# A hybrid attention block on one core: norm weights turned by PE, and two loads of x issued by ScalarE

## The reference

```python
def _rmsnorm(x, g, eps=1e-6):
    y = x * lax.rsqrt(jnp.mean(x * x, axis=-1, keepdims=True) + eps)
    return y * g

h = _rmsnorm(x, norm_g[layer])               # x (512, 2048), norm_g (2048)
proj = h @ w_in[layer]                       # w_in (2048, 10304)
aq, ak, av, ag, cq, ckv, kr, bg, mg = jnp.split(proj, SPLIT_POINTS, axis=-1)
oa = _diff_attention(...)                    # 8 heads, values of 128
oa = _rmsnorm(oa, a_subln_g[layer], 1e-5) * (1.0 - lam_init)       # a_subln_g (128)
ya = (oa * silu(ag)) @ w_oa[layer]
q  = _rmsnorm(cq,  q_norm_g[layer])  @ w_uq[layer]                 # q_norm_g (512)
kv = _rmsnorm(ckv, kv_norm_g[layer]) @ w_ukv[layer]                # kv_norm_g (512)
ob = _mla_attention(...)
yb = (ob * silu(bg)) @ w_ob[layer]
merged = sigmoid(ga) * ya + sigmoid(gb) * yb
x = x + merged @ w_out[layer]
return _rmsnorm(x, final_g)
```

## Time and profile before

| | us |
|---|---|
| median of 3 runs | 1429.9 (1429.22 to 1430.29) |
| profiled execution, whole | 1429.3 |
| its span, first to last instruction | 1427.5 |
| PE busy | 1413.2 (99% of the span) |
| DVE busy | 1020.0 (71%) |
| ACT busy | 707.1 (50%) |
| POOL busy | 31.5 (2%) |

### The profile page before, as it was taken

How to read it: one execution, slowest core, us unless ns; L and a number is a source line. 1 busy time by engine, 2 the same in 40 slices (tenths; PEclk the granted TensorE clock), 3 DMA queues, 4 the chain that set the end, 5 groups by cost and what they waited for, 6 DMA issues and landing times.

```text
span 1427.5 us, 17881 instructions
## 1 busy us (share of the span) xinstructions
PE 1413.2 (99%) x6604; PEld 1175.1 (82%) x6604; DVE 1020.0 (71%) x1381; ACT 707.1 (50%) x894; POOL 31.5 (2%) x52
## 2 busy tenths in 40 slices
PE   8999999999999999999999999999999999999997
PEld 7888888888888888888888878888888888888886
DVE  6967898798878868677667656666676353478966
ACT  6546334544344456665666667555564222324434
POOL 0000000000000000000000000000000000000000
PEclk9999999999999999999999999999999999999999
DMA  8439576766756543222222434322242444617674
GB/s 300 145 125 316 177 263 186 236 213 212 238 184 207 184 146 83 79 82 81 81 81 82 114 106 133 84 72 66 81 140 74 151 125 152 207 45 247 197 254 172
DMA packets 182976, 218.43 MB, mean 153 GB/s; under 512 B 19456, under 2 KB 133248, under 8 KB 182272
## 3 DMA queue, kind: packets, MB, share of 16 engines
q1 hardware_dynamic: 174304, 197.64, 44.5%
q10 hardware_dynamic: 8608, 19.93, 3.6%
HBM read 195.51 MB, written 22.02 MB: 152 GB/s over the span
## 4 chain that ended last, share of the span: by engine, by line
PE 91%; DVE 3%; DMA 1%; ACT 1%; issue 1%; SPq 1%; POOL 0%; DVEq 0%; POOLq 0%; ACTq 0%
PE duo L2115 28%; PE duo L2117 28%; PE duo L2116 28%; PE duo L2168 2%; DMA start_y<-start_columns 1%; PE duo L2142 1%; PE duo L2145 1%; SPq L610 1%; ACT m_hi L886 1%; PE duo L2159 1%; PE duo L2164 1%; PE duo L2163 1%; PE duo L2160 1%; PE duo L2161 1%; PE duo L2598 0%
## 5 line engine op out<-in xcount | busy, mean ns | idle before, releaser
L1385 DVE TENSOR_TENSOR w_lo<-w_raw,w_hi 128x1024 fp32r<-128x1024 f32 (+1 forms) x116 | 135.3, 1167 | 99.3 <-ACT w_hi L781 98.7
L2115 PE MATMUL duo<-h_hi,w_hi 128*128 128x512 f32 x512 | 201.8, 394 | 0.0
L2117 PE MATMUL duo<-h_hi,w_lo 128*128 128x512 f32 x512 | 199.6, 390 | 0.0
L2116 PE MATMUL duo<-h_lo,w_hi 128*128 128x512 f32 x512 | 199.6, 390 | 0.0
L886 ACT ACTIVATE m_hi<-m_raw 128x2048 fp32r<-128x2048 f32 (+1 forms) x66 | 115.5, 1752 | 144.6 <-PE duo L2117 71.5
L781 ACT ACTIVATE w_hi<-w_raw 128x1024 fp32r<-128x1024 f32 (+1 forms) x118 | 119.2, 1011 | 124.3 <-DMA w_raw<-in_w_ob_dram 65.8
L1502 DVE TENSOR_TENSOR m_lo<-m_raw,m_hi 128x2048 fp32r<-128x2048 f32 (+3 forms) x71 | 141.9, 2001 | 26.9 <-ACT m_hi L886 26.5
L2115 PE MATMUL duo<-m_hi,h_hi 128*128 128x512 f32 x368 | 144.6, 393 | 1.6 <-DVE h_lo L1538 0.9
L2117 PE MATMUL duo<-m_hi,h_lo 128*128 128x512 f32 x368 | 143.3, 389 | 0.0
L2115 PE MATMUL duo<-m_hi,s_hi 128*128 128x512 f32 x320 | 124.5, 389 | 0.0
L2117 PE MATMUL duo<-m_hi,s_lo 128*128 128x512 f32 x320 | 124.5, 389 | 0.0
(11 more groups left out here) (322 smaller groups left out, 2991.0 us busy)
## 6 DMA issues: line engine op xcount, KB each, us to landing
m_raw<-in_w_in_dram SPq DMA_DIRECT2D x110, 512.0 KB, 4.7
w_raw<-in_w_in_dram SPq DMA_DIRECT2D x132, 256.0 KB, 3.0
o_raw<-in_w_out_dram SPq DMA_DIRECT2D x32, 512.0 KB, 5.1
spare<-in_w_in_dram SPq DMA_DIRECT2D x17, 512.0 KB, 4.6
h_raw<-in_w_in_dram SPq DMA_DIRECT2D x17, 512.0 KB, 4.9
w_raw<-in_w_oa_dram SPq DMA_DIRECT2D x32, 256.0 KB, 3.3
sig<-gates SPq DMA_DIRECT2D x8, 1024.0 KB, 6.3
w_raw<-in_w_ob_dram SPq DMA_DIRECT2D x32, 256.0 KB, 3.4
```

The source lines that it names most:

```text
L1385: dve.tensor_tensor(w_lo[:, piece.slot, 0:cols], w_raw[:, piece.slot, 0:cols], w_hi[:, piece.slot, 0:cols].bitcast(F32), ALU.subtract).the ...
L2115: pe.matmul(dst, lhs_hi, rhs_hi, start=start, stop=False)
L2116: pe.matmul(dst, lhs_hi, rhs_lo, start=False, stop=False)
L2117: return pe.matmul(dst, lhs_lo, rhs_hi, start=False, stop=stop)
```

## The change

The four norm weights are loaded as rows into a new tile `g_rows` (25 rows of 128 values: 16 of `norm_g`, 4 and 4 of the two inner norms, 1 of the sub-norm). ACT issues these four loads. PE turns the 25 rows to columns in one product with the identity, behind the 20 products of the warm-up and ahead of the first turns of x, into a bank of PSUM; DVE copies the 25 columns into their places in `small`, ahead of its first norm of x. The waits for the gains' loads become waits for the turn (DVE's copy) and for the copy (ACT's first `unit_hi`, DVE's first `part_lo`).

The second halves of tiles 0 and 1 of x are issued by ACT, as its first instructions, and no longer by SP. SP's queue loses these two and the four loads of the gains.

```diff
+X_BY_ACT = (1, 3)
+GAINS = KT + 2 * LT + 1
...
+        g_rows = at("g_rows", 184, [P, P])
...
-        g_sub = small[:, 24:25]
+        g_sub_raw = small[:, 24:25]
+        gains = small[:, 0:GAINS]
...
-        g_sub_raw = small[:, 132:133]
+        g_sub = small[:, 132:133]
...
             for i, (t, cols) in enumerate(X_PARTS):
                 if i == X_SPLIT + 2:
                     merge_piece(0)
-                    with nc.allow_non_contiguous_dma("gains by partition"):
-                        sp.dma_start(g_in, norm_g[0, :].rearrange("(t p) -> p t", p=P)).then_inc(g_in_in, 16)
                     merge_piece(1)
                     merge_piece(2)
-                sp.dma_start(x_tok_in[:, X_HOME[t], cols], x[0, t * P:(t + 1) * P, cols]).then_inc(x_in[i], 16)
+                if i not in X_BY_ACT:
+                    sp.dma_start(x_tok_in[:, X_HOME[t], cols], x[0, t * P:(t + 1) * P, cols]).then_inc(x_in[i], 16)
             merge_piece(OWN_RAW - 1)
-            with nc.allow_non_contiguous_dma("gains by partition"):
-                for dst, src in ((g_q, q_norm_g), (g_kv, kv_norm_g), (g_sub_raw, a_subln_g)):
-                    sp.dma_start(dst, src[0, :].rearrange("(t p) -> p t", p=P)).then_inc(gains_in, 16)
...
+            for i in X_BY_ACT:
+                t, cols = X_PARTS[i]
+                act.dma_start(x_tok_in[:, X_HOME[t], cols], x[0, t * P:(t + 1) * P, cols]).then_inc(x_in[i], 16)
+            for r0, n, src in ((0, KT, norm_g), (KT, LT, q_norm_g), (KT + LT, LT, kv_norm_g), (KT + 2 * LT, 1, a_subln_g)):
+                act.dma_start(g_rows[r0:r0 + n, :], src[0, :].rearrange("(t p) -> t p", p=P)).then_inc(rows_in, 16)
             act.wait_ge(ones_set, 5)
             act.activation(f_sum[:, 0:1], ones, ACT.Square)
             for i in range(4):
                 square_x(i)
             half_hi(0, 0)
-            act.wait_ge(g_in_in, 16)
+            act.wait_ge(gains_ready, 1)
             unit_hi(0)
...
-            act.wait_ge(gains_in, 16 * 3)
...
+            dve.wait_ge(rows_turned, 1)
+            dve.tensor_copy(gains, bank[1][:, 0:GAINS]).then_inc(gains_ready, 1)
             norm_tile(0)
             norm_tile(1)
-            dve.wait_ge(g_in_in, 16)
+            dve.wait_ge(gains_ready, 1)
...
-                    dve.wait_ge(gains_in, 16 * 3)
...
             for _ in range(WARM_UP):
                 pe.matmul(bank[0][:, 0:P], ident, ident, start=True, stop=True)
+            pe.wait_ge(rows_in, 16 * 4)
+            pe.transpose(bank[1][:, 0:GAINS], g_rows[0:GAINS, :], ident[0:GAINS, 0:GAINS]).then_inc(rows_turned, 1)
             pe.wait_ge(x_normed, 1)
```

More of the change, by code:

```diff
@@ L397, in hybrid_encoder @@
         used = sem("used")
-        g_in_in, gains_in, lambdas_in = sem("g_in_in"), sem("gains_in"), sem("lambdas_in")
+        rows_in, rows_turned, gains_ready, lambdas_in = (
+            sem("rows_in"), sem("rows_turned"), sem("gains_ready"), sem("lambdas_in"))
         x_in = [sem(f"x_in{i}") for i in range(len(X_PARTS))]
```

## The result

The changed kernel takes 1433.67 us (median of 8 runs, 1432.19 to 1435.35); the kernel before took 1429.97 us beside it (8 runs, 1429.22 to 1430.57). The ratio is 1.0025, 95% interval [1.0016, 1.0035]: slower by a quarter of a per cent, 3.7 us. The forecast was 1433.0 us (1430.5 to 1435.4). A few executions far outside the rest (1567.93 to 2905.23 us) are left out of the medians in this document.

The account below looks back on a forecast made before the run. PE bounds the kernel, busy 1395.81 of 1397.77 us after 22.03, so delays before that pass on almost whole. Held copy +1.3 and late constants +1.8 gave +3.1: 1432.4, or 1433.0 us against the median (range 1430.5 to 1435.4).

Parts of the forecast that it names:

- held copy: At the start, DVE's norms wait for the gains' copy behind PE's warm-up: second weight step +1.3 us (+1.0 to +1.7).
- the weights that are no longer late: Before PE's second weight step: the second weight tile arrives sooner, giving back at most 0.4 us.
- a first real product 6.8 us after the warm-up's end: Sign on PE at the start: this gap is 6.8 us, where it had been 5.1.
- late constants: At the start, x on ACT's queue delays cst; PE starts at 4.6, not 2.59 us: +1.8 us.
- a clock that rises at the same instant: Case for PE's warm-up with cst late: clock rise unmoved, warm-up ends near 11.1 us, 1.1 late.
- one that rises as long after the start: Case for PE's warm-up with cst late: clock rise delayed equally, warm-up ends 2.0 us late.
- That the two add: At the start: every later step hangs on the copy, so +1.3 and +1.8 sum to +3.1 us.
- Rival 2: PE's pause before the first turns drops the clock; 2.5 us lost, 1435.5 with cst late, 1433.5 without; chance 0.15.
- Rival 1: At the start: cst not delayed, PE starts near 2.6, sum +1.3 less clock savings, about 1431.0 us; chance 0.28.
- Rival 3: At the start: early weights pay, clock rises early, PE gains 0.4 us and more, about 1429.0 us; chance 0.05.
- from there to the last matmul the same 1397.8 us: Sign on PE: from first weights of step two to the last matmul, the length stays 1397.8 us.
- nothing later can absorb or repay it: PE after 22.03 us: busy 1395.81 of 1397.77 us, so earlier delays or gains pass on almost whole.

Follow-up runs that it names:

- experiment 7: The changed kernel again, unedited, for a second profiled execution; median 1433.47 us, ratio 1.0022.
- experiment 8: The kernel before again, unedited, for a second profiled execution; median 1430.20 us, ratio 1.0000.
- experiment 12: Changed kernel with one product behind the first turns replaced by a 25-column turn of the identity, restoring PE's old 6604 passes; 1433.13 us, ratio 1.0020.
- experiment 2: Kernel before with only the second halves of x tiles 0 and 1 moved to ACT's queue, gains loaded as before; 1430.96 us, ratio 1.0006.
- experiment 1: Changed kernel with all halves of x issued by SP again, gains still as rows from ACT; 1432.39 us, ratio 1.0014.
- experiment 5: Changed kernel with ACT's six loads issued behind its table load and first square instead of ahead; 1432.79 us, ratio 1.0017.
- experiment 3: Changed kernel with DVE's copy of the gains moved behind the norms of tiles 0 and 1; 1431.99 us, ratio 1.0012.
- experiment 10: Kernel of experiment 6 with one product behind the first turns replaced by a turn of the identity, restoring 6604 PE passes; 1430.22 us, ratio 1.0001.
- experiment 6: Changed kernel with x all on SP, gains turned behind the first turns of x and copied behind the two norms; 1431.21 us, ratio 1.0005.
- experiment 9: Kernel before with one more small, unused product on PE behind the first turns of x; 1431.55 us, ratio 1.0011.
- experiment 4: Changed kernel with ten more identity products on PE behind the turn of the gains; 1432.66 us, ratio 1.0017.
- experiment 11: Kernel of experiment 6 with the four by-column gain loads back on SP's queue, into an unread buffer; 1432.08 us, ratio 1.0015.

## Why the prediction was right, and where it was not

**The held copy (+1.3): right in its mechanism, somewhat too large.** Turn, copy and norm follow the warm-up's end as worked out: 0.2 us to the copy, 1.2 more to the norm, 1.35 to the turns. What was too large is the last step. The forecast let step two begin where the turns of a unit end (21.63 in the earlier trace rows); they overlap with the next product, which begins 0.35 us after the turns' start (24.43, 24.78). So the weights that are no longer late give 0.65 us back and not 0.41. The sign named for it, a first real product 6.8 us after the warm-up's end, came out at 6.82 in experiment 7 (11.44 to 18.26). Between the two executions at the medians (experiments 7 and 8) the head is 2.14 longer, of which the warm-up's end is 1.09 (10.35 to 11.44), and the copy the other 1.05.

**The late constants (+1.8): the place is right, the size depends on the execution.** PE started at 4.54, against the 4.6 worked out from the packets of the earlier trace rows. That it agrees so closely is in part luck: by the stretch from 2.2 to 3.6 us a row of x takes an engine some 0.21 us (an estimate: 67.7% of 16 engines over 1.4 us, 72 rows) and not the 0.33 that the forecast took, but the engines also stand idle for 18% of it. The Trainium skill, "DMA: Bandwidth & Descriptors", section "Queues, rings and completion order", has whole packets of nine to seventeen descriptors go at a time; by it the constants would have landed at 2.6 or, behind eight rows of x at the forecast's 0.33 us, at 5.2 (an estimate). The landing at 4.50 to 4.88 in the six profiles with the halves of x issued at 0.74 us lies between. The rows of the constants begin to move all the way from 1.74 to 4.02 us in the changed kernel, 62 of them beside 72 rows of x between 2.2 and 3.6, so this trace shows rows in turn, or very small batches, and neither of the two. From there the forecast took 1.8, between a clock that rises at the same instant (1.1) and one that rises as long after the start (2.0). In the first two profiles of the changed kernel it was 1.08 and 1.09 (against 10.03 and 10.35, the two of before), and with the edit of experiment 12, 12.41 - 10.03 = 2.4. Both cases occur.

**That the two add: only through the copy.** Late constants alone cost 0.7 of the head (experiment 2, 0.3 against the second execution of before), the held copy alone 0.6 (experiment 1, 0.3 likewise), and both together 2.1 to 2.75. Undoing either one brings the head down by 0.5 to 2.1 (experiments 5, 1, 3; the smallest is experiment 5, whose fallen clock took 1.5 us of the gain). The forecast had this right where it said that every later step moves along because all hang on the copy.

**Rival 2, the clock falls back: it happens, and was priced too high.** The forecast gave it 0.15 and 2.5 us. The granted clock fell to 0.50 in two of the five profiles in which PE waits 2.56 us before the first turns of x (the first of the changed kernel and experiment 5, not experiments 1, 7 and 12). It comes back after 3.4 us. By the time from first turns to first real product (4.09 us in experiment 7) the loss is 0.6 us in the first of the changed kernel (4.70), where the clock fell 1.4 us after the turns began, and 1.5 in experiment 5 (5.61), where it fell after 0.5. The Trainium skill, "TensorE: Matmul & The Clock Gate", section "HAM oscillation — how this bites in real kernels", describes waits of PE between bursts of products that bring the lower clock back. The 0.50 from 15.25 to 18.67 us agrees with it in kind, but behind the same wait the clock stayed up in three profiles of five.

**Rivals 1 and 3: wrong.** cst was delayed in every profile with the halves of x issued at 0.74 us. The early weights gave their 0.65 us, but under a head that was late already.

**The step that failed: "from there to the last matmul the same 1397.8 us", and "nothing later can absorb or repay it".** The length behind the head was taken for fixed, since no wait on PE there was for a load. In the execution at the median it is 1399.69. The forecast costed the turn of the gains as one product on PE that overlaps the warm-up's last pass, and did not count that it makes PE's program longer. With that one product a packet of code moves ahead of the end of a load of output weights some 1,290 us later; VectorE gets the weights 1.6 to 2.1 us later (the two executions of the changed kernel, experiments 10 and 6, before and experiment 9), and PE waits for it. That the product makes the loss is shown by experiments 9 and 10 on the kernels without the two costs at the head; that it does so through the packet is argued from the table, and in the changed kernel itself experiment 12 took back only 0.3 to 0.5 us. So 1433.0 is near 1433.67 partly by luck: the head was put at +3.1 and measured +2.1 to 2.75, and 1.3 us, by experiments 7 and 8, came from a place where nothing was expected.

**What stays open.** Why an execution of the same program can have the packet at either place (the first and second of the changed kernel). Why the load lands 1.6 us and more later beside a packet of 0.93 us: counted in the trace, SyncE's last rows of 2048 bytes move after 1307.0 us in experiment 9 and before 1305.0 in experiment 10, so some engine is behind by more than the one packet. The packet was moved only through the length of PE's program, never by itself. And how far the head of the changed kernel varies between executions: 24.51 and 24.78 in two profiles, 25.64 in experiment 12.

## What to carry to other kernels

A wait that is put first on an engine costs nothing only while what it waits for is early; look at what the awaited engine has in front of it (here twenty warm-up products) and put the wait behind the work that doesn't need it: moving two lines gave back 1.7 of the 3.7 us. A small load that everything hangs on wants the DMA engines to itself, so a large load on a second queue should go out a little behind it, not in the same instant. And where a kernel is bound by one engine for over a thousand microseconds, compare more than one profiled execution of each version at its median, and try the same change with the instruction count of the bound engine unchanged, before a difference of 0.1% is put down to the change.

## What the runs showed that was not expected

- One product of 25 columns, far off the path and used by nothing, made a kernel of 1430 us slower by 1.6 us (ratio 1.0011 [1.0002, 1.0020]).
- On the queue "instruction" q8 packets of 16 KB move all through an execution, 41 of them (42 in experiment 4); the one near the output weights holds a DMA engine for 0.93 us. Where it lies among loads that PE waits for goes with 1.6 to 2.1 us in the landing of one of them.
- A load of 65 KB landed 1.95 us later (4.54 instead of 2.59) because 0.5 MB on another queue was issued in the same instant; issued 0.36 us later (1.10 us) the larger load left it alone (2.73).
- The warm-up ended between 8.9 and 12.4 us, since the granted clock rose anywhere from 5.9 to 10.8. Where the norms don't wait for the warm-up and the constants are early (both executions of before, experiments 6 and 9 to 11), its end lay between 9.2 and 10.35 and the head between 22.03 and 22.37. In the changed kernel the end of the warm-up is passed on in full: 11.44 and 24.51 in experiment 7, 12.41 and 25.64 in experiment 12.
